# Two-block transformer kernel on one core: the mLSTM layer's q, k, v and o projections as pairs of seven quarter products, with the heads' ScalarE work at fixed products

## What is computed

```python
proj = h @ w_in                       # (512 x 1024) @ (1024 x 3088)
qk = silu(causal_conv(proj[..., :1024], conv_w, conv_b))      # 4 taps
q, k = split_heads(qk[..., :512]), split_heads(qk[..., 512:]) * 64 ** -0.5
v = split_heads(proj[..., 1024:2048])
o = proj[..., 2048:3072]
gates = proj[..., 3072:]              # input and forget gate of each head
hh = mlstm_chunkwise(q, k, v, i_pre, f_pre)    # decayed attention, divided by max(|den|, exp(-m))
hh = head_rmsnorm(hh, norm_w) * sigmoid(o)
return hh @ w_out
```

## Time and profile before

| | |
|---|---|
| median of 3 runs | 2070.03 us (2070.0 to 2078.05) |
| profiled execution, its own time | 2064.82 us |
| its span | 2062.9 us, mean granted TensorE clock 0.986 |
| TensorE busy over the span | 2012.4 us (98%) |
| VectorE, ScalarE, GpSimd busy over the span | 842.8, 579.2, 510.0 us |
| the second layer's projections and heads | 343 to 554 us of the span |

### The profile page before, as it was taken

The page is one execution under the profiler, slowest core; times in us unless marked ns, Lnnn a source line. Parts: engine busy times, 40 slices in busy tenths (PEclk is TensorE's granted clock), DMA queues, the critical chain, the costliest instruction groups (busy, mean ns, idle before and its releaser), DMA issues. The chain is left out here.

```text
span 2062.9 us, 27646 instructions
## 1 busy us (share of the span) xinstructions
PE 2012.4 (98%) x10854; PEld 1611.6 (78%) x10854; DVE 842.8 (41%) x1151; ACT 579.2 (28%) x1072; POOL 510.0 (25%) x450
## 2 busy tenths in 40 slices
PE   8999998999999999999999999999999999999997
PEld 7878654666547888888866676764999999999996
DVE  3898586366635444444233555651300000000023
ACT  1433114344412111110056577631211211111101
POOL 5665230111114333335313333321300000000011
PEclk9999998999999999999999999999999999999998
DMA  8214821322124656522121111100967577778883
GB/s 321 76 51 174 305 96 42 96 66 78 57 79 155 207 203 213 192 85 87 67 82 62 52 52 53 51 21 17 291 212 244 185 244 259 240 250 300 326 329 142
DMA packets 82736, 312.67 MB, mean 152 GB/s; under 512 B 10152, under 2 KB 10672, under 8 KB 82480
## 3 DMA queue, kind: packets, MB, share of 16 engines
q1 hardware_dynamic: 75952, 289.73, 40.3%
q0 software_dynamic: 4320, 13.76, 2.1%
q10 hardware_dynamic: 2336, 7.40, 1.0%
HBM read 301.49 MB, written 9.36 MB: 151 GB/s over the span
## 5 line engine op out<-in xcount | busy, mean ns | idle before, releaser
L2801 PE MATMUL banks<-sb_act,sb_ring 128*128 128x192 f32 (+3 forms) x3696 | 500.6, 298 | 1.7 <-DMA sb_ring<-in_w_moe_up 0.9
L2801 PEld LDWEIGHTS banks<-sb_act,sb_ring 128*128 128x128 f32 x3696 | 498.3, 191 | 2.7 <-DMA sb_ring<-in_w_moe_up 1.3
L257 PE MATMUL banks<-sb_x_norm,sb_ring 128*128 128x512 f32 x624 | 277.3, 599 | 2.0 <-ACT sb_x_norm L642 2.0
L3085 DVE TENSOR_TENSOR sb_act<-sb_work,banks 128x128 f32<-128x128 f32 (+3 forms) x88 | 27.7, 315 | 505.3 <-PE banks L2801 499.5
L257 PEld LDWEIGHTS banks<-sb_x_norm,sb_ring 128*128 128x128 f32 x624 | 117.1, 192 | 138.4 <-issue 136.2
L287 PE MATMUL banks<-sb_x_norm,sb_ring 128*128 128x256 f32 x840 | 197.4, 381 | 1.6 <-ACT sb_ring L450 1.5
L287 PEld LDWEIGHTS banks<-sb_x_norm,sb_ring 128*128 128x128 f32 x840 | 158.1, 190 | 25.6 <-issue 4.8
L2668 POOL DMA_INDIRECT sb_work<-first_expert_rows,sb_table x8 | 7.5, 935 | 465.0 <-DMA first_expert_rows<-sb_x_norm 462.9
L268 PEld LDWEIGHTS banks<-sb_ring,sb_x_norm 128*128 128x128 f32 x1024 | 116.1, 192 | 2.4 <-issue 1.0
L268 PE MATMUL banks<-sb_ring,sb_x_norm 128*128 128x128 f32 x1024 | 117.3, 275 | 0.0
L1493 PE MATMUL banks<-sb_act,sb_ring 128*128 128x512 f32 x256 | 112.4, 594 | 0.4 <-DVE sb_act L2456 0.4
(11 more groups left out here) (460 smaller groups left out, 2805.6 us busy)
## 6 DMA issues: line engine op xcount, KB each, us to landing
sb_ring<-in_w_moe_up SPq DMA_DIRECT2D x176, 512.0 KB, 4.6
sb_ring<-in_w_moe_down SPq DMA_DIRECT2D x64, 704.0 KB, 5.8
sb_act<-in_cond_w SPq DMA_DIRECT2D x84, 512.0 KB, 4.1
sb_ring<-in_w_ffn_up SPq DMA_DIRECT2D x44, 512.0 KB, 4.9
sb_ring<-in_w_h_in SPq DMA_DIRECT2D x32, 512.0 KB, 3.5
sb_ring<-in_w_in SPq DMA_DIRECT2D x28, 512.0 KB, 6.1
sb_ring<-in_w_m_in SPq DMA_DIRECT2D x24, 512.0 KB, 3.6
sb_ring<-in_w_ffn_down SPq DMA_DIRECT2D x16, 704.0 KB, 5.3
```

What stands on the lines that cost most here:

```text
L257: last = m.nc.tensor.matmul(bank[:, 0:act.shape[2]], w[:, rows(k, P)], act[:, k, :], start=(k == 0), stop=(k == kt - 1))
L2801: last = nc.tensor.matmul(ps[:, b % BANKS, 0:cap], w, act, start=(k == 0), stop=(k == kt - 1))
L3085: nc.vector.tensor_tensor(hid[:, j, 0:cap], silu_t[j % 2][:, 0:cap], ps[:, (2 * j + 1) % BANKS, 0:cap], ALU.mult).then_inc(m.evac, 2)
```

## The change

The first blocks of q and k stay classical. The other 22 blocks become 11 pairs, (q1, k1), (v0, v1), (o0, o1) and so on, each seven quarter products. TensorE does 12 products ahead of head 0 and then 8, 9, 9, 10, 9, 9, 8 and 3 beside the heads (`M_BESIDE`), of which up to four before the totals (`M_TOTALS`). ScalarE's work for a head is put at fixed indices of these products: the root of head h - 2 (`M_ROOT`), the two halves of the decays (`M_DECAY`, `M_DECAY2`), the silus (`M_CONV`) and the square of head h - 1 (`M_SQUARE`), each behind the `keep` of that product. VectorE makes the four sums of the input around the gate rows, and `edges(h + 1)` now stands between the weights of head h and the division of head h - 1. GpSimd makes the differences and additions beside its work for the heads. The product for v pairs is `multiply_tokens` (L292), 16 records of 128x128 in place of 8 of 128x256. Tiles are laid out anew: q and k of two blocks at a time, o of four.

```diff
 
-M_FIRST = [("q", 0), ("k", 0), ("v", 0), ("o", 0)]
-M_BESIDE = [[("v", 1), ("q", 1), ("k", 1)], [("o", 1), ("v", 2), ("q", 2)], [("v", 3), ("k", 2), ("o", 2)],
-            [("o", 3), ("v", 4), ("q", 3)], [("v", 5), ("k", 3), ("o", 4)], [("o", 5), ("v", 6)], [("o", 6), ("v", 7)],
-            [("o", 7)]]
-M_BLOCKS = M_FIRST + [block for beside in M_BESIDE for block in beside]
+M_FIRST = [("q", 0), ("k", 0)]
+M_PAIRS = [(("q", 1), ("k", 1)), (("v", 0), ("v", 1)), (("o", 0), ("o", 1)), (("q", 2), ("k", 2)), (("v", 2), ("v", 3)),
+           (("o", 2), ("o", 3)), (("q", 3), ("k", 3)), (("v", 4), ("v", 5)), (("o", 4), ("o", 5)), (("v", 6), ("v", 7)),
+           (("o", 6), ("o", 7))]
+M_BLOCKS = M_FIRST + [block for pair in M_PAIRS for block in pair]
+M_AHEAD, M_BESIDE, M_TOTALS = 12, [8, 9, 9, 10, 9, 9, 8, 3], 4
...
     cT = W[:, 13, 0:ST * HEADS].rearrange("p (t h) -> p t h", h=HEADS)
     probs, den, dec = (W[:, 0:4, :], A[:, 26:30, :]), W[:, 4, :], W[:, 6:10, :]
     values = A[:, 8:16, :]
-    raw = lambda n: A[:, 24 + n % 2, :]
+    raw = lambda n: A[:, (24 if n // 2 % 2 else 14) + n % 2, :]
     convs = [name for name in M_BLOCKS if name[0] in "qk"]
-    qk_tile = lambda kind, j: A[:, j + 4 * (kind == "k"), :]
+    qk_tile = lambda kind, j: A[:, j % 2 + 4 * (kind == "k"), :]
+    o_tile = lambda h: A[:, 16 + h % 4, :]
+    halves = lambda t: t.rearrange("p a (b c) -> p (a b) c", c=HALF)
+    pairs = Pairs(m, plan, len(M_FIRST), len(M_PAIRS), m.HN,
+                  [halves(t) for t in (A[:, 2:4, :], A[:, 6:8, :], A[:, 20:22, :], A[:, 22:24, :])],
+                  lambda j: tuple(ps[:, bank, 0:HALF] for bank in ((0, 1, 5), (5, 1, 0))[j % 2]), True,
+                  tokens=[j for j, pair in enumerate(M_PAIRS) if pair[0][0] == "v"])
+    tile_of = {"q": lambda h: raw(2 * h), "k": lambda h: raw(2 * h + 1), "v": lambda h: values[:, h, :], "o": o_tile}
+    tiles = lambda j: tuple(tile_of[kind](h) for kind, h in M_PAIRS[j])
+    begun = lambda h: M_AHEAD + sum(M_BESIDE[:h])
+    beside = lambda h: [divmod(n, 7) for n in range(begun(h), begun(h + 1))]
+    convolved = {h: M_PAIRS[3 * h // 2] for h in (0, 2, 4)}
...
         def _(pe):
-            by_feature, by_token = by_features(m, m.HN, KD), by_tokens(m, m.HN, KD, ST)
-
-            def project(kind, h):
-                b = at[kind, h]
-                s = b % SLOTS
-                pe.wait_ge(m.loaded[s], 16 * (plan.uses[s] + b // SLOTS + 1))
-                if b >= 2:
-                    pe.wait_ge(m.evac, plan.done + b - 1)
-                (by_token if kind == "v" else by_feature)(ps[:, b % 2, :], m.ring[:, s, :]).then_inc(m.blocks_done, 1)
+            go = lambda n: pairs.multiply(pe, n)
 
             def totals(h):
 
@@ -1581,14 +1587,15 @@
                 last = nc.tensor.matmul(ps[:, 0, :], m.ring[:, 0, rows(k, P)], m.HN[:, k, :], start=(k == 0),
                                         stop=(k == KD - 1))
             last.then_inc(m.blocks_done, 1)
-            project(*M_FIRST[1])
-            project(*M_FIRST[2])
-            project(*M_FIRST[3])
+            pe.wait_ge(m.loaded[1], 16 * (plan.uses[1] + 1))
+            by_features(m, m.HN, KD)(ps[:, 1, :], m.ring[:, 1, :]).then_inc(m.blocks_done, 1)
+            go(7)
             pe.wait_ge(c_ready, 1)
             for t in range(ST):
                 last = nc.tensor.transpose(ps[:, 6, rows(t, HEADS)], g["i"][:, rows(t, P)],
                                            m.c("ident")[0:HEADS, 0:HEADS])
             last.then_inc(cT_ready, 1)
+            go(M_AHEAD - 7)
 
             for h in range(HEADS):
                 lo = 64 * (h % 2)
@@ -1599,14 +1606,14 @@
                     last = nc.tensor.matmul(scores[i], qk_tile("k", h // 2)[lo:lo + 64, rows(i, P)],
                                             qk_tile("q", h // 2)[lo:lo + 64, i * P:], start=True, stop=True)
                 last.then_inc(score, 1)
-                project(*M_BESIDE[h][0])
+                ahead = min(M_TOTALS, M_BESIDE[h])
+                go(ahead)
                 if h:
                     totals(h - 1)
-                for name in M_BESIDE[h][1:]:
-                    project(*name)
+                go(M_BESIDE[h] - ahead)
                 if h == HEADS - 1:
                     pe.wait_ge(head_out, EARLY)
-                    pe.wait_ge(m.evac, plan.done + plan.n - 1)
+                    pe.wait_ge(m.evac, plan.done + plan.n)
                     out_piece(m, pe, out, values, 0, range(0, EARLY))
                 if h:
                     norms[h - 1].pe(m, pe)
@@ -1632,10 +1639,31 @@
...
+            def take_pair(j):
+                kind, h = M_PAIRS[j][0]
+                how = ACT.Sigmoid if kind == "o" else ACT.Copy
+                a, b = tiles(j)
+                act.wait_ge(m.added, pairs.added_no(j, C21))
+                act.wait_ge(m.blocks_done, pairs.blocks_no(j))
+                last = nc.scalar.activation(b[:, LO], pairs.banks(j)[0], how)
+                if kind == "o":
+                    step(last)
+                    step(nc.scalar.activation(b[:, HI], b[:, HI], how))
+                    last = nc.scalar.activation(a, a, how)
+                last.then_inc(m.evac, 2)
+
+            def keep(j, i):
+                kind, h = M_PAIRS[j][0]
+                if i + 1 == P2 and kind == "o" and h >= 4:
+                    act.wait_ge(head_out, h - 2)
+                which = {P1: (pairs.OF_1,), P7: (pairs.OF_7,), P6: (pairs.OF_16,), P2: (pairs.OF_2,),
+                         P5: (pairs.OF_165,), P4: (pairs.OF_74,)}
+                for part in which.get(i + 1, ()):
+                    pairs.keep(act, j, part, tiles(j))
+                if i + 1 == P3:
+                    take_pair(j)
 
             def conv_silu(kind, j):
                 n = convs.index((kind, j))
...
             step(nc.scalar.activation(g["t"], g["t"], ACT.Exp, scale=-1.0))
             give(act, nc.scalar.activation(g["t"], g["t"], ACT.Ln, bias=m.c("one")[0:HEADS, :]), gate_soft, 1)
             take("k", 0)
-            conv_silu("q", 0)
+            for i in range(4):
+                keep(0, i)
             act.wait_ge(floor_log, 1)
             give(act, nc.scalar.activation(g["f"], g["m"], ACT.Exp, scale=-1.0), floor_out, 1)
-            take("v", 0)
+            for n in range(4, 7):
+                keep(0, n)
+            for n in range(3):
+                keep(1, n)
+            conv_silu("q", 0)
             conv_silu("k", 0)
-            take("o", 0)
+            for n in range(10, M_AHEAD):
+                keep(*divmod(n, 7))
+
+            def decays(h, first, last):
+                act.wait_ge(edge, h + 1)
+                for i in range(first, last):
+                    c = cT[:, i, h:h + 1]
+                    exp = nc.scalar.activation(dec[:, i, rows(i, P)], dec[:, i, rows(i, P)], ACT.Exp, bias=c)
+                    if i < ST - 1:
+                        step(exp)
+                        step(nc.scalar.activation(dec[:, i, (i + 1) * P:], max_of[:, h % 2, (i + 1) * P:], ACT.Exp, bias=c))
+                    else:
+                        give(act, exp, decay, h + 1)
 
             for h in range(HEADS):
-                act.wait_ge(edge, h + 1)
-                for i in range(ST):
-                    c = cT[:, i, h:h + 1]
-                    last = nc.scalar.activation(dec[:, i, rows(i, P)], dec[:, i, rows(i, P)], ACT.Exp, bias=c)
-                    if i < ST - 1:
-                        step(last)
-                        step(nc.scalar.activation(dec[:, i, (i + 1) * P:], max_of[:, h % 2, (i + 1) * P:], ACT.Exp, bias=c))
-                give(act, last, decay, h + 1)
-                for name in M_BESIDE[h - 1] if h else ():
-                    if name[0] in "qk":
-                        conv_silu(*name)
-                for name in M_BESIDE[h][0:2]:
-                    take(*name)
-                if h:
-                    norms[h - 1].square(m, act)
-                for name in M_BESIDE[h][2:]:
-                    take(*name)
-                if h:
-                    norms[h - 1].root(m, act)
+                for n, (j, i) in enumerate(beside(h)):
+                    keep(j, i)
+                    if n == M_ROOT[h]:
+                        norms[h - 2].root(m, act)
+                    if n == M_DECAY[h]:
+                        decays(h, 0, 2)
+                    if n == M_DECAY2[h]:
+                        decays(h, 2, ST)
+                    if n == M_CONV[h]:
+                        for name in convolved[h - 1]:
+                            conv_silu(*name)
+                    if n == M_SQUARE[h]:
+                        norms[h - 1].square(m, act)
+            norms[HEADS - 2].root(m, act)
             norms[HEADS - 1].act(m, act)
             for k in range(KD):
                 act.wait_ge(m.evac, out.done + k + 1)
...
                          keys_added, (ST - 1) * h + i)
 
+            def beside_product(j, i):
+                part = i + 1
```

(44 more changed lines are left out.)

11 lines of the change are left out of this document (5 added, 6 removed).

## The result

| | changed kernel | before, same chip |
|---|---|---|
| median | 2104.55 us (2100.76 to 2112.04, 4 runs) | 2070.02 us (2068.02 to 2078.05) |
| ratio | 1.0161, 95% interval 1.0144 to 1.0179 | |
| profiled execution, its span | 2100.76 us, 2099.0 us | 2064.82 us, 2062.9 us |

The change makes the kernel 34.5 us slower. The prediction was +8 us with a range up to 2091, so the sign of its sum was right and its size far too small, outside the range. The profiled execution of the kernel before is not one of the four in its column and is 5 us shorter than their median; that of the changed kernel is the shortest of its four.

What follows compares the result with a forecast made beforehand. TensorE's issue was taken to bound the stretch: 29.2 us new idle less 5.2 old and 19.1 gained is +4.9, plus 1.5 contention and 1.7 clock, about +8 us: 2078, range 2064 to 2091.

Steps and rivals of the forecast that it cites:

- The gain, 19.1 us: TensorE's seven quarter products per pair in place of classical blocks: 19.1 us less on the path.
- Rival 4: Products take 1.89 us, not the 1.73 pitch: 12 us less gain, 2090; 7% together with GpSimd becoming the bound.
- The waits, 29.2 us: New TensorE idle at the start and in heads 0 to 7, mostly before the norm's matmul: 29.2 us.
- 0.16 us of drained pipe: Drained-pipe cost of 0.16 us for each of TensorE's four present waits, making their 4.6 us 5.2.
- The table loads: ScalarE's function table loads cost 1.28 us, the next ACTIVATE within 0.02; counting 2.66 would lose about 5 us more.
- Rival 1: Division ends by each head's last product, so tails stay hidden: -14.5 us, 2055.5, or 2060 with some idle; 13%.
- Contention, 1.5 us: VectorE's two-input SBUF operations (edges, half the finish) slowed beside GpSimd: 1.5 us, bounds nothing and 4.
- GpSimd as the bound: Rival: GpSimd's differences late after each wait for a head, +20 to +25 us, 2092; 7% together with the pitch rival.
- The clock, 1.7 us, bound 7: Half clock on TensorE after long waits: 1.7 us for head 7 alone, bounds 0 and 7 for four waits.
- the row at 623 us: Old profile's clock at 0.50 after short waits: 32 matmuls take 15.6 us against 13.9, priced as 1.7 us.
- its own signs of being wrong: VectorE idle ahead of the square, TensorE waiting for GpSimd's differences, pitch over 1.73, or half clock after each wait.
- Rival 2: Contention and clock at their upper bounds: +16 us, 2086, or 2089 with late GpSimd sums; 29%.

Runs made afterwards that it cites:

- The last version: Changed kernel with earlier decays, norm put off, GpSimd's first differences held for the gate rows, head 7's decays in head 6, its weights after the division: 2050.12 us, 0.9921.
- edit 6: Changed kernel with GpSimd's first differences held back at the layer's start, until the last scaled input tile (1.0148) or the gate rows (1.0147).
- fill: Changed kernel plus unused spare matmuls ahead of the norm's matmul in heads 1, 3, 4 and 7: 2093.17 us, 1.0105.
- fill_all: Changed kernel plus unused spare matmuls ahead of the norm's matmul in all of heads 1 to 7: 2084.41 us, 1.0055.
- edges: Changed kernel with the next head's edge additions put back behind the division on VectorE: 2085.84 us, 1.0086.
- tail: Changed kernel with a second piece of the output projection ahead of the norm's matmul in head 7: 2103.31 us, 1.0145.
- start: Changed kernel with GpSimd's first four differences held until VectorE has scaled the last input tile: 2103.53 us, 1.0148.
- gate: Changed kernel with GpSimd's first differences held until VectorE has made the gate rows: 2101.65 us, 1.0147.

## Why the prediction was wrong

- *The gain, 19.1 us*: right. The pitch is 1.73 us for a product of q, k or o, and 1.79 for one of v. The last version, whose waits are about as short as those before the change (4.1 and 4.6 us), has a layer 19.0 us shorter than before. Rival 4 (the pitch) is out.
- *The waits, 29.2 us*: right in place and releaser, and nearly in size. Head by head predicted and measured: start 0.9 and 0.8, head 0 0.8 and 0.7, heads 1 to 7 4.5, 1.2, 4.1, 4.5, 2.2, 2.1, 8.9 and 5.9, 1.05, 4.2, 5.9, 1.9, 2.0, 9.0 (2.51 + 5.58 + 0.87). Only heads 1 and 4 were too low, by 1.4 each, and that is the contention of the next point. The prediction took 0.16 us of drained pipe off for each old wait and did not add it for the eleven new ones; with it the sum is 33.2, 4.0 more. The table loads took 1.28 us here too, with the next ACTIVATE within 0.02 (four of them from 570.29 to 580.05 us). Rival 1 (tails hidden) is out.
- *Contention, 1.5 us*: half of what it was on the chain, 3.1 us. The edges of heads 1 and 4 took 2.75 and 2.85 us in place of 1.27, each 1.5 more, where the bound taken was 0.57 a head; those of head 3 took 1.27, and the median of all 32 additions stayed at 0.29. The 3.1 us lie inside the waits of heads 1 and 4 and are not to be added again. It missed the place where VectorE and GpSimd meet first, ahead of the layer: 2.0 us (edit 6).
- *GpSimd as the bound*: out. It was busy 104.6 us of 244, its differences took 1.30 us on average in this stretch, not 1.60, and TensorE has no wait for it among the rows above.
- *The clock, 1.7 us, bound 7*: **this is the step that failed**, on two counts. The prediction took head 7's fall alone, "the other three are between dense stretches, as the present ones"; three of the four falls came just there. And each was priced by the row at 623 us, which holds 1.7 us of excess; these stretches last 10 to 14 us at 0.50 and cost 3.8 to 5.7 us. Together they are 18.9 us, and the run with spare matmuls in every head gives 18.2 for it by itself. The row at 623 us was not wrong, but one short fall in another surrounding was made the upper bound of all. The prediction had named the half clock after each wait among its own signs of being wrong. The scores of head 4, set for 468 us, began at 479.41.

Between the two marks of the layer: 4.9 forecast, 4.0 more idle time, 18.9 clock are 27.8 of 29.1 us; 1.3 are not placed. The 3.9 us ahead of the layer are the 2.0 of the way in and 1.9 that are there before it, where L1331 starts at 317.6 to 322.9 us in the thirteen profiles and so differs from run to run. The same holds for the 3.1 us behind: the profile of before had the shortest of the thirteen.

Rival 2 (contention and clock at their bounds) named the cause, and its 2086 to 2089 was still too low, for the same reason.

*What stays open*: when the clock falls. It fell after waits of 5.90, 4.16, 5.86 and 5.58 us, and of 3.96, 3.89, 3.10, 2.98, 2.87, 2.38, 2.00, 1.97 and 1.88; it did not after 3.11, 2.28, 2.04, 1.61 and 1.05, nor after 1.88 in the changed kernel itself. The wait ahead of the output piece shows it best: 2.51 us in seven of the kernels, with a fall in fill and fill_all (12 records in 6.99 and 7.08 us) and none in changed, edges, tail, start and gate (12 in 5.39, tail 24 in 10.54), though TensorE's program in the 14.4 us ahead of it is the same in all. What it did before that differs, and no run here shows what decides.
